# Expert weights loaded, waited for and given back in two halves, and another order of the shared expert's products

## What is computed

```python
s = sigmoid(h @ w_router)                         # 384 x 64
combine = weights of the top 6 experts per token  # out of the best 4 of 8 groups
gu = einsum("td,edf->tef", h, w_expert_gu)        # 64 experts, 1024 -> 2 x 256
act = silu(gu[..., :256]) * gu[..., 256:] * combine[..., None]
routed = einsum("tef,efd->td", act, w_expert_down)   # 256 -> 1024
gs = h @ w_shared_gu
shared = (silu(gs[..., :256]) * gs[..., 256:]) @ w_shared_down
return routed + shared
```

## Time and profile before

| | us |
|---|---|
| median of 3 runs | 767.47 (766.24 to 767.67) |
| the profiled execution | 770.51 |
| its span in the profile | 768.4 |
| PE busy | 703.7 (92%) |
| DVE busy | 406.0 (53%) |
| ACT busy | 190.3 (25%) |
| POOL busy | 84.9 (11%) |
| bytes moved | 259.15 MB, mean 337 GB/s |

### The profile page before, as it was taken

The page is one execution under the profiler, slowest core; times in us unless marked ns, Lnnn a source line. Parts: engine busy times, 40 slices in busy tenths (PEclk is TensorE's granted clock), DMA queues, the critical chain, the costliest instruction groups (busy, mean ns, idle before and its releaser), DMA issues.

```text
span 768.4 us, 11388 instructions
## 1 busy us (share of the span) xinstructions
PE 703.7 (92%) x4241; PEld 407.0 (53%) x4241; DVE 406.0 (53%) x1004; ACT 190.3 (25%) x320; POOL 84.9 (11%) x49
## 2 busy tenths in 40 slices
PE   1579999899989989999999999999999989999795
PEld 1579888688856545544444444444444435443232
DVE  3178999467095653455543545455444364334144
ACT  3135423564274112121121111211211111111013
POOL 2234544511400100000000000000000000000000
PEclk9979999989999999999999999999999999999898
DMA  9997566713679439789999999999999999999962
GB/s 324 374 385 250 207 231 219 285 46 100 202 266 429 210 134 392 296 329 382 429 424 423 423 426 421 427 422 426 423 429 426 422 424 426 426 426 423 422 264 95
DMA packets 47548, 259.15 MB, mean 337 GB/s; under 512 B 6272, under 2 KB 8928, under 8 KB 30464
## 3 DMA queue, kind: packets, MB, share of 16 engines
q1 hardware_dynamic: 39504, 249.05, 80.1%
q0 software_dynamic: 1808, 5.92, 2.2%
q10 hardware_dynamic: 6176, 3.40, 1.5%
HBM read 254.64 MB, written 3.71 MB: 336 GB/s over the span
## 4 chain that ended last, share of the span: by engine, by line
PE 65%; DMA 18%; DVE 11%; ACT 3%; issue 1%; SPq 1%; DVEq 0%; ACTq 0%
PE psum L2042 20%; DMA w_gu<-in_w_expert_gu 14%; PE psum L2054 9%; PE psum L1936 8%; PE psum L2017 6%; PE psum L529 4%; PE psum L530 4%; PE psum L531 4%; DVE psum L1117 3%; PE psum L1917 3%; DMA w_gu<-in_w_in 2%; DMA w_gu<-in_w_ada 2%; DVE f_acc L1526 2%; PE psum L1948 1%; PE psum L2004 1%
## 5 line engine op out<-in xcount | busy, mean ns | idle before, releaser
L2042 PE MATMUL psum<-w_gu,hgT 128*32 128x512 f32 (+1 forms) x1280 | 193.2, 601 | 10.7 <-DMA w_gu<-in_w_expert_gu 10.7
L2042 PEld LDWEIGHTS psum<-w_gu,hgT 128*32 128x32 f32 (+1 forms) x1280 | 59.5, 120 | 136.9 <-issue 136.8
L1526 DVE TENSOR_TENSOR f_acc<-f_acc,psum 128x512 f32<-128x512 f32 x156 | 106.1, 687 | 45.6 <-PE psum L2017 42.4
L2054 PE MATMUL psum<-w_dn,actT 128*32 128x512 f32 (+1 forms) x640 | 100.2, 602 | 0.5 <-ACT actT L938 0.5
L1511 DVE SCALAR_TENSOR_TENSOR act<-sil,wsl,psum 128x256 f32<-128x256 f32 x27 | 18.3, 677 | 134.9 <-ACT sil L963 130.2
L2017 PE MATMUL psum<-y_hi,onehotT 128*128 128x512 f32 x156 | 67.8, 434 | 4.6 <-DVE f_acc L1526 2.5
L524 POOL TENSOR_TENSOR w_lo<-w_gu,w_hi 128x2048 fp32r<-128x2048 f32 x14 | 64.6, 4616 | 62.7 <-ACT w_hi L727 62.7
L1936 PE MATMUL psum<-onehot,h_hi 128*128 128x512 f32 (+1 forms) x168 | 67.7, 403 | 0.0
L1936 PE MATMUL psum<-onehot,h_lo 128*128 128x512 f32 (+1 forms) x168 | 64.9, 386 | 0.0
L1517 DVE TENSOR_TENSOR y_lo<-psum,y_hi 128x1024 fp32r<-128x1024 f32 x27 | 33.0, 1224 | 56.0 <-ACT y_hi L967 56.0
L2017 PE MATMUL psum<-y_lo,onehotT 128*128 128x512 f32 x156 | 61.3, 393 | 0.0
(11 more groups left out here) (293 smaller groups left out, 867.2 us busy)
## 6 DMA issues: line engine op xcount, KB each, us to landing
w_gu<-in_w_expert_gu SPq DMA_DIRECT2D x64, 2048.0 KB, 19.7
w_dn<-in_w_expert_down SPq DMA_DIRECT2D x64, 1024.0 KB, 19.2
w_gu<-in_w_ada SPq DMA_DIRECT2D x12, 2048.0 KB, 16.2
w_gu<-in_w_in SPq DMA_DIRECT2D x4, 2048.0 KB, 8.7
w_gu<-in_w_out SPq DMA_DIRECT2D x2, 2048.0 KB, 9.7
bc<-mod_rows POOLq DMA_DIRECT2D x6, 512.0 KB, 7.4
w_gu<-in_w_in SPq DMA_DIRECT2D x2, 1024.0 KB, 15.3
w_gu<-in_w_shared_gu SPq DMA_DIRECT2D x1, 2048.0 KB, 9.6
```

What stands on the lines that cost most here:

```text
L1526: v.tensor_tensor(dst, dst, bank(5 + n), ALU.add).then_inc(f_added, 1)
L2042: ins = t.matmul(bank(2)[rows, :], column(c)[:, rows], w_gu[s][:, c, :], start=(c == 0), stop=(c == NC - 1), tile_position=(0, rows.start))
L2054: ins = t.matmul(bank(3 + n)[rows, :], actT[:, j, rows], w_dn[s][:, j, 512 * n:512 * (n + 1)], start=(j == 0), stop=(j == 1), tile_positio ...
```

## The change

It has two parts. First, an order on TensorE: sh_down(1) goes ahead of the rank product, and sh_down(2) moves out of the first products to behind gate_up of group 0. VectorE's f_first(2) and the one-hot tile of group 1 of batch 1 go behind group 0's act accordingly, and SP issues w_dn[3] behind group 0's gate/up refills.

Second, each w_gu is loaded in two transfers of 1 MB (chunks 0 to 3, chunks 4 to 7). The first half counts on a semaphore of its own, gu_first. gate_up waits for the first halves before chunk 0 and for the second before chunk 4, and gives each half back after its last product, so gu_used counts two per use. SP loads first halves of all of a group's refills, then second halves. The rest of the diff fits the counts to that.

```diff
@@ SP
-                sp.dma_start(w_gu[e][:, :, :], w_egu[e]).then_inc(gu_in[e], 16)
-                if dn_base(e):
-                    sp.wait_ge(dn_used[e], dn_base(e))
-                sp.dma_start(w_dn[e][:, :, :], w_edn[e]).then_inc(dn_in[e], 16)
+                for h in HALF:
+                    sp.dma_start(w_gu[e][:, h, :], w_egu[e, :, h, :]).then_inc(gu_half(e, h), 16)
+                if not dn_base(e):
+                    sp.dma_start(w_dn[e][:, :, :], w_edn[e]).then_inc(dn_in[e], 16)
...
-                for n, e in chosen_e.items():
-                    s = n % SLOTS
-                    sp.wait_ge(gu_used[s], pre(s) + n // SLOTS)
-                    sp.dma_start(w_gu[s][:, :, :], (w_egu[e:e + 1] if LOADS[n] < FIXED else w_egu[bass.ds(e, 1)]).rearrange("e p c n -> p (e c) n"))\
-                        .then_inc(gu_in[s], 16)
+                for half, h in enumerate(HALF):
+                    for n, e in chosen_e.items():
+                        s = n % SLOTS
+                        sp.wait_ge(gu_used[s], pre(s) + (2 * (n // SLOTS) - 1 + half))
+                        src = w_egu[e:e + 1, :, h, :] if LOADS[n] < FIXED else w_egu[bass.ds(e, 1), :, h, :]
+                        sp.dma_start(w_gu[s][:, h, :], src.rearrange("e p c n -> p (e c) n"))\
+                            .then_inc(gu_half(s, h), 16)
+                if k == 0:
+                    late = PSLOTS - 1
+                    sp.wait_ge(dn_used[late], dn_base(late))
+                    sp.dma_start(w_dn[late][:, :, :], w_edn[late]).then_inc(dn_in[late], 16)
@@ ScalarE
-                a.wait_ge(gu_used[s_last], loads)
+                a.wait_ge(gu_used[s_last], loads * 2 + pre(s_last))
@@ VectorE
-            f_first(2)
             for g in range(3):
                 tokens_of(3, g, g, parts_of(g))
-            for j in range(2):
-                make_onehot(1, j)
+            make_onehot(1, 0)
...
                 if k == 0:
+                    make_onehot(1, 1)
+                    f_first(2)
                     make_onehot(1, 2)
@@ TensorE
             sh_down(0)
             transposes(2, act_s)
+            sh_down(1)
             t.wait_ge(beaten_ready, 1)
             t.wait_ge(a_ready, 3)
             t.matmul(bank(4, 0, NE), ones[0:NE, :], beaten[:, :], start=True, stop=True).then_inc(rank_done, 1)
-            sh_down(1)
             transposes(3, act_s)
...
-            for c in range(NC // 2):
-                gather(0, c)
-            sh_down(2)
-            for c in range(NC // 2, NC):
+            for c in range(NC):
                 gather(0, c)
...
-                for s, loads in uses:
-                    t.wait_ge(gu_in[s], loads * 16)
                 for c in range(NC):
+                    if c % (NC // 2) == 0:
+                        for s, loads in uses:
+                            if c == 0:
+                                t.wait_ge(gu_first[s], loads * 16)
+                            else:
+                                t.wait_ge(gu_in[s], loads * 16 + 16 * pre(s))
                     for s, rows, last in tiles:
                         ins = t.matmul(bank(2)[rows, :], column(c)[:, rows], w_gu[s][:, c, :],
                                        start=(c == 0), stop=(c == NC - 1), tile_position=(0, rows.start))
-                        if c == NC - 1 and last:
+                        if c in (NC // 2 - 1, NC - 1) and last:
                             ins.then_inc(gu_used[s], 1)
...
+                if k == 0:
+                    sh_down(2)
                 transposes(k + (NT + 1), act)
```

More of the change, by code:

```diff
@@ L363, in build_layer @@
         state_in, router_in, grow2_in = sem("state_in"), sem("router_in"), sem("grow2_in")
+        gu_first = [sem(f"gu_first{s}") for s in range(SLOTS)]
         gu_in = [sem(f"gu_in{s}") for s in range(SLOTS)]
@@ L455, in loads_of @@
             return len(range(s, NE, SLOTS))
-        OVER_LOADS = PRE + loads_of(0)
-        assert all(pre(s) + loads_of(s) == OVER_LOADS for s in range(4))
+        assert all(pre(s) == PRE and loads_of(s) == loads_of(0) for s in range(4))
         def chunk_source(name):
@@ L571, in load_wait, with gu_half @@
         def load_wait(n):
-            return n % SLOTS, pre(n % SLOTS) + 1 + n // SLOTS
+            return n % SLOTS, 1 + n // SLOTS
         first_load = [sum(len(g) for g in PLAN[:k]) for k in range(GROUPS + 1)]
+        HALF = (slice(0, NC // 2), slice(NC // 2, NC))
+        def gu_half(s, h):
+            return gu_first[s] if h is HALF[0] else gu_in[s]
         def refills(k):
@@ L673, in over_pair @@
                     e = sp.value_load(table_e[0:1, bass.ds(jj * 4 + (NE + s), 1)], min_val=0, max_val=NE - 1)
[L674 to L677, removed]
+                    sp.wait_ge(gu_used[s], jj * 2 + (PRE + 2 * loads_of(s)))
+                    for h in HALF:
+                        sp.dma_start(w_gu[s][:, h, :], w_egu[bass.ds(e, 1), :, h, :].rearrange("e p c n -> p (e c) n"))\
+                            .then_inc(gu_half(s, h), 16)
+                    sp.wait_ge(dn_used[s], jj + (loads_of(s) + dn_base(s)))
                     sp.dma_start(w_dn[s][:, :, :], w_edn[bass.ds(e, 1)].rearrange("e p j n -> p (e j) n"))\
@@ L965, in y_high @@
             def y_high(s_last, loads):
-                a.wait_ge(dn_used[s_last], loads + (dn_base(s_last) - pre(s_last)))
+                a.wait_ge(dn_used[s_last], loads + dn_base(s_last))
                 a.activation(y_hi[:, :], bank(3, 0, 1024), ACT.Copy).then_inc(yhi_ready, 1)
@@ L984, in over @@
                 p = jj * 2 + (GROUPS + q)
-                loads = jj + (OVER_LOADS + 1)
+                loads = jj + (loads_of(0) + 1)
                 for n in range(2):
@@ L2049, in down @@
                 for s, loads in uses:
-                    t.wait_ge(dn_in[s], (loads + (dn_base(s) - pre(s))) * 16)
+                    t.wait_ge(dn_in[s], (loads + dn_base(s)) * 16)
                 for n in range(2):
```

## The result

| | us |
|---|---|
| before, median of 7 | 767.23 (765.98 to 770.39) |
| after, median of 7 | 762.65 (761.08 to 764.3) |
| ratio after to before | 0.9945, 95% interval 0.9925 to 0.9966 |
| profiled execution, before and after | 770.51, 762.65 |
| its span, before and after | 768.4, 760.6 |

The change makes the kernel faster by 4.6 us (2.6 to 5.8 by the interval). The forecast was 757.5 us, a gain of 10.0. The direction and the order of events were right; more than half of the gain is missing.

What follows compares the result with a forecast made beforehand. TensorE was taken to lead until about 600 us, then the transfer stream; starting it 6.5 us earlier and leaving 3.5 us behind the last landing gave 10.0 us, median 757.5, range 752.5 to 764.

Steps and rivals of the forecast that it cites:

- The stream bounds the end, the last group too: Group 26's gate/up weights land 0.2 us before use, so transfers bound the last group though no wait is shown.
- Order on TensorE, 5.0 us: Early TensorE work: moving sh_down(1) and sh_down(2) ends group 0's down product at 286.3 instead of 291.3, 5.0 us earlier.
- VectorE's moved work, w_dn[3], SP's longer queue: hidden: Around groups 0 and 1: later one-hots, the later w_dn[3] load and 59 more SP transfers cost TensorE nothing.
- The stream full 6.5 us earlier: Around groups 3 and 4: the transfer stream starts its full run 5.8 to 6.8 us earlier, 6.5 taken.
- 3.5 us behind the last landing instead of 7.0: Last gate/up: with halves, only 3.5 us of work remain behind the last landing, not 7.0.
- The wait in the middle: nothing: Inside each gate/up: the added wait costs 0.04 us, at most 0.12, swallowed by group 25's remaining wait.
- More transfers on a full stream: zero taken, 5.5 us kept for the range: After 350 us: 51 added transfers cost zero, at most 0.11 us each, 5.5 us in all.
- (a): Rival, full stream: a small gap per transfer, up to 0.11 us, leaves 4.5 us gain, 758.5 to 763 us; chance 0.12.
- (b): Rival, full stream: uncovered gap per transfer makes it slower, 775 us at 0.35 us each, some 855 in series; chance 0.12.
- (d): Rival, late gate/ups: halves bring nothing, only the stream's 5.0 to 6.5 us remain, 761 to 762.5; chance 0.10.
- (c): Rival, expert stage: stream faster or its lead larger, TensorE alone bounds, 17.9 us less wait costs, 751 to 753; chance 0.08.
- (e): Rival, early order: saves 2 us less as the rank or VectorE's moved work is late, 759 to 760; chance 0.08.

Runs made afterwards that it cites:

- the order alone: The change's new TensorE order with every w_gu whole, one 2 MB transfer, against the kernel before: 763.76 us against 767.15, ratio 0.9962.
- The second and third profiles of the kernel before: The unchanged kernel before, run twice more for further profiled executions: 767.93 and 769.04 us.
- the kernel with rows kept: Kernel before with each w_gu loaded by two transfers, even and odd partitions, rows still 16 KB: 768.15 us against 767.45, ratio 1.0.
- both parts: The whole change, order and halves, built like the other follow-up kernels, against the kernel before: 761.39 us, ratio 0.9927.
- The late halves: New order with only the last 8 of 64 loads in halves, against the kernel before: 760.78 us, ratio 0.989.
- four transfers: The whole change with each half loaded by two transfers, four of 0.5 MB per w_gu, rows of 4 KB: 769.84 us against 767.45 before.

## Why the prediction was right in its order and wrong in its size

Its steps, one by one:

1. **The stream bounds the end, the last group too.** Right. In the order alone group 26 shows a wait of 0.59 us where the forecast had worked out 0.2 us of slack. The second and third profiles of the kernel before show one too, 0.30 and 0.34 us.
2. **Order on TensorE, 5.0 us.** The steps are right: first products at 260.26 (forecast 261.2 - 1.3 = 259.9, with what came from ahead), sh_down(2) in the gap, act under it. Of the 5.0 us, 1.7 were the down product's 5.35 against 3.65. Against the profiles of the kernel before the stage of the order alone is 4.8 us shorter, so for them the term holds; but its median is only 3.4 us lower, and 5.0 lies outside the interval. With the term left out the order is worth 3.3 us, and the profiles without the drop give 3.5. This fits if many executions of the kernel before don't pay the term. An estimate speaks for it: the earliest issue in the table (212.2), the shortest stage of the kernel before (528.1), the 24.9 us behind it and 2.1 outside the span make 767.3 us, yet 23 of the 58 executions of that kernel took less than 767.0. None of the three profiles is of such an execution, so it isn't shown.
3. **VectorE's moved work, w_dn[3], SP's longer queue: hidden.** Right; TensorE shows no wait for them.
4. **The stream full 6.5 us earlier.** Right, counted in bytes. From 260 to 400 us the core took in 339 GB/s and not 317, which is 3.1 MB more or 7.2 us of the stream; 1.3 of these come from ahead of the change, and the lower rate had already taken about 0.5 us back. The start itself is thus 7.2 - 1.3 + 0.5 = 6.4 us earlier.
5. **3.5 us behind the last landing instead of 7.0.** Right: 3.65 us from the last wait to the end in the change's profile. In that of both parts, with group 25's slow half, 4.1 us are left behind the last landing (730.4 to 734.5), and the stage is 0.1 us longer. The late halves by themselves gained 3.3 us by the medians and 2.5 by the profiles.
6. **The wait in the middle: nothing.** Right where the wait is met: such groups run in one piece of 7.04 to 7.09 us, as before. Where TensorE does wait, the two halves take 3.64 or 3.65 us each, together 0.2 us more than in one piece.
7. **More transfers on a full stream: zero taken, 5.5 us kept for the range.** This is the step that failed: "I take zero, since the w_dn loads are nearest". The runs showed 3.4 to 3.6 us in its place. The bound was good and the value not. (The 0.29 us of its working are 0.28 by the same rows; that changes nothing.) w_dn moves in 1 MB transfers of 8 KB rows inside the 425 GB/s, but it does so before and after; that a mean contains such transfers doesn't say what they cost in it. From the landings: group 25's second halves were due at 712.4 - 1.3 = 711.1 and landed at 714.5, group 26's were due at 728.4 and landed at 731.9: 3.4 and 3.5 us late, and group 20's, earlier in the stream, 2.5 (624.15 against 621.6). 1% of the 380 us of full stream is 3.6 us. Of the rivals, (a) holds in mechanism, with the price on rows and not on transfers, as the kernel with rows kept shows. (b), a fixed part paid in series, is refuted by the same kernel: 64 transfers more cost 0.0% there, with an interval of 0.24% to both sides, 1.8 us, where (b) needs 10 and more. The Trainium skill ("DMA: Bandwidth & Descriptors", Anatomy of one DMA) gives about 2.0 us fixed per DMA, for those that GpSimd issues, and doesn't say that they are paid in series; here, where SP issues them into a full queue, they are not. (d), that the halves bring nothing, has nearly the time that was measured, 761 to 762.5; but the order alone took 763.76 us and both parts 761.39, and in the profile the first halves are used before the second ones land. (c) is out, since TensorE still waits 10.3 us for weights, and (e), since its order came out as forecast.

Together: 10.0 - 3.5 = 6.5 us, and that is what the two profiled executions show behind the shared expert's down weights (743.45 - 215.39 = 528.1 us before, 735.69 - 214.10 = 521.6 after). The medians have 4.6 us, and 5.8 in the second comparison. Less the 1.7 us of the clock drop 6.5 would be 4.8; that this is where the rest went is likely by step 2, and not shown.

There was one more weakness in how the sum was joined to the median. The profiled execution of before took 3.0 us more than the median, and the gain was subtracted from both alike. Part of what it had more were drops of the clock ahead of the change. TensorE's granted clock in that execution, in windows ahead of everything that the change touches, and in the second profile of the same kernel:

```profile
150.00:160.00 10.00, 8.57 (x51) 7.36 (x51) 4.33 (x14) 7.94 (x21) 3.43 (x1) 0.84 0.62 230
160.00:170.00 10.00, 10.00 (x63) 9.26 (x64) 7.34 (x27) 5.41 (x21) 0.00 (x0) 0.82 0.01 2
```

```profile
150.00:160.00 10.00, 7.97 (x58) 6.92 (x58) 4.39 (x14) 8.51 (x21) 3.43 (x1) 1.00 0.70 259
160.00:170.00 10.00, 10.00 (x74) 8.75 (x73) 9.52 (x37) 6.62 (x24) 0.00 (x0) 1.00 0.01 2
```

0.84 and 0.82 against 1.00 and 1.00, in the stage of the mLSTM products; the shared expert's down weights are issued 2.6 us earlier in the second (212.81 against 215.39). So 2.6 us of what it had more lay there and had nothing to do with the change. The drop in group 0's down product is in both.

## What to carry to other kernels

A load cut for earlier use cost, on a full stream of transfers, by the rows that it added, and not by being one transfer more. So cut only the loads that gain by it, at the start of that stretch and the last ones behind which work remains, and leave the rest whole: here that saved 9.1 us, and cutting them all 4.6 to 5.8. A mean rate that holds small pieces does not show that they are free: compare rates with and without them. And a duration that rests on a lowered clock should be seen in more than one execution before it becomes a term of a sum, and even three profiles may not stand for the median.

## What the runs showed of the hardware that I had not expected

The price of rows: 0.07 us per 128 rows more on the full stream of 16 engines, the same, within the rounding, from 16 KB to 8 KB as from there to 4 KB. The trace's records of single packets agree: from 400 to 660 us the median packet of 16 KB takes 614 ns on its engine and that of 8 KB 313 (kernel before), and one of 4 KB 161 (four transfers). Two packets of half the length thus take 12 and 9 ns more than one. The number of transfers has no price that can be measured.

SP's issue of a transfer takes 0.33 us mostly. A set of six spans 4.79 us at 346.66; the six issues are 2.0 of it, and the rest is mostly SP's waits for the second halves' slots. But in the last third of the kernel after, such sets span far more (start, duration, line, count):

```profile
588.89 10.04 SPq L665 DMA_DIRECT2D w_gu<-in_w_expert_gu  x6
...
623.81 13.65 SPq L665 DMA_DIRECT2D w_gu<-in_w_expert_gu  x6
```

The single issues are longer there: in the second of these sets their median is 1.99 us and the longest 6.1, and the lone x at 709.55 takes 6.19 where it took 0.36 before. The transfers of that set land 25 to 30 us after their issue, those of the set at 346.66 after 6 to 16. So the long issues come with a long queue; that the queue is their cause is not shown. The stream stays full meanwhile (1.01).
